# A weight ring of twelve slots of 1 MB in place of six of 2 MB, in an encoder step with 32 experts

## The reference

```python
logits = xt @ w_router + b_router              # 288 x 32
top_val, top_idx = lax.top_k(logits, 4)
gates = softmax weights of the four, 0 elsewhere
for e in range(32):
    gu = xt @ w1[e] + b1[e]                    # w1[e]: 1024 x 2048
    gate = minimum(gu[:, :1024], 7.0)
    up = clip(gu[:, 1024:], -7.0, 7.0)
    act = (up + 1) * (gate * sigmoid(1.702 * gate))
    out = out + gates[:, e:e+1] * (act @ w2[e] + b2[e])   # w2[e]: 1024 x 1024
y = layer_norm(alpha * h1 + out)
```

## Time and profile before

| | |
|---|---|
| three timed runs | 1148.43, 1148.84, 1150.51 us (median 1148.84) |
| profiled execution | 1148.38 us, its span 1146.6 us |
| mean granted PE clock | 0.98 of full speed |
| read from HBM | 420.11 MB |
| PE, DVE, ACT busy | 93%, 36%, 17% of the span |
| ring loads | 192 DMAs of 2 MB |

### The profile page before, as it was taken

One profiled execution on the slowest core, in us unless ns is written; L12 is line 12 of the kernel. 1 busy time (PEld: TensorE's weight loads), 2 busy tenths in 40 slices (PEclk: granted clock), 3 DMA queues, 4 the chain that ended last, 5 costly groups with the idle time before them and its releaser, 6 DMA issues.

```text
span 1146.6 us, 13983 instructions
## 1 busy us (share of the span) xinstructions
PE 1063.8 (93%) x5419; PEld 449.5 (39%) x5420; DVE 407.4 (36%) x692; ACT 193.9 (17%) x432; POOL 17.1 (1%) x25
## 2 busy tenths in 40 slices
PE   8989999889999999999999999999999999999992
PEld 7766565333333333333333333333333333333340
DVE  7683256422222222222222222222222222222227
ACT  3334110111111111111111111111111111111102
POOL 1003000000000000000000000000000000000001
PEclk9999897999999999999999999999999999999997
DMA  9650243999999999999999999999999999999971
GB/s 324 258 221 1 76 183 132 374 386 428 429 429 428 428 428 429 429 430 427 429 428 428 429 429 430 427 429 428 428 429 429 430 426 429 428 428 429 429 297 41
DMA packets 37201, 421.91 MB, mean 368 GB/s; under 512 B 6285, under 2 KB 6925, under 8 KB 12506
## 3 DMA queue, kind: packets, MB, share of 16 engines
q1 hardware_dynamic: 36842, 420.41, 87.4%
q10 hardware_dynamic: 336, 1.18, 0.3%
HBM read 420.11 MB, written 1.46 MB: 368 GB/s over the span
## 4 chain that ended last, share of the span: by engine, by line
DMA 45%; PE 43%; DVE 9%; issue 1%; ACT 1%; SPq 0%; DVEq 0%; ACTq 0%
DMA ring<-in_w_dram 44%; PE ps L817 20%; PE ps L839 7%; PE ps L548 4%; PE ps L662 3%; DVE area L1469 1%; PE ps L859 1%; PE ps L527 1%; PE ps L645 1%; DVE area L1460 1%; DVE area L1463 1%; DVE area L1456 1%; DVE stats L1179 1%; PE ps L762 1%; PE ps L798 1%
## 5 line engine op out<-in xcount | busy, mean ns | idle before, releaser
L817 PE MATMUL ps<-ring,area 128*64 128x512 f32 x2048 | 453.1, 596 | 24.8 <-DMA ring<-in_w_dram 24.0
L817 PEld LDWEIGHTS ps<-ring,area 128*64 128x64 f32 x2048 | 142.0, 137 | 316.1 <-issue 256.2
L839 PE MATMUL ps<-ring,area 128*64 128x512 f32 x1024 | 232.2, 595 | 0.0
L1456 DVE TENSOR_SCALAR area<-ps 128x512 f32<-128x512 f32 x32 | 22.1, 691 | 382.5 <-PE ps L817 382.5
L1469 DVE TENSOR_TENSOR area<-area,ps 128x1024 f32<-128x1024 f32 (+1 forms) x99 | 120.2, 1214 | 57.1 <-PE ps L859 57.1
L839 PEld LDWEIGHTS ps<-ring,area 128*64 128x64 f32 x1024 | 69.7, 136 | 124.5 <-issue 122.1
L1115 ACT ACTIVATE area<-area 128x512 f32<-128x512 f32 x32 | 20.1, 629 | 494.5 <-DVE area L1456 494.5
L859 PE MATMUL ps<-y_sb,giveT 128*128 128x512 f32 x198 | 71.4, 443 | 14.7 <-DVE area L1469 12.3
L1448 DVE SCALAR_TENSOR_TENSOR y_sb<-ps,gcol,y_sb 64x512 fp32r<-64x512 f32 x64 | 48.1, 751 | 101.6 <-ACT y_sb L1087 101.2
L789 PE MATMUL ps<-area 128*64 128x512 bf16 x558 | 66.1, 382 | 2.2 <-DVE area L1383 2.2
L1087 ACT ACTIVATE y_sb<-ps,gcol 64x512 fp32r<-64x512 f32 x64 | 43.8, 684 | 95.4 <-PE ps L839 94.6
(11 more groups left out here) (199 smaller groups left out, 608.6 us busy)
## 6 DMA issues: line engine op xcount, KB each, us to landing
ring<-in_w_dram SPq DMA_DIRECT2D x192, 2048.0 KB, 22.0
area<-in_w_o_dram SPq DMA_DIRECT2D x1, 4096.0 KB, 13.0
area<-in_w_in_dram SPq DMA_DIRECT2D x1, 2560.0 KB, 16.4
area<-in_w_in_dram SPq DMA_DIRECT2D x1, 2336.0 KB, 9.3
area<-in_w_in_dram SPq DMA_DIRECT2D x1, 2048.0 KB, 20.4
lnb<-in_ln_g_dram SPq DMA_DIRECT2D x3, 512.0 KB, 10.3
lnb<-in_ln_b_dram SPq DMA_DIRECT2D x3, 512.0 KB, 11.7
rows<-in_x_prompt_dram SPq DMA_DIRECT2D x2, 512.0 KB, 3.9
```

The source lines that it names most:

```text
L817: last = mm(ps_gu[g * BLK:(g + 1) * BLK, c, :], x[:, spot(k), :], w[:, a:a + 512], start=False, stop=(k == KT - 1))
L839: last = mm(ps_y[g * BLK:(g + 1) * BLK, :], hT[:, c, h, :], w2_t[:, h, c, g * 512:(g + 1) * 512], start=False, stop=(h == 1 and c == 3))
L1456: v.tensor_scalar(g_sb, ps_gu[:, 0, :], LIMIT, None, ALU.min).then_inc(gate, 1)
```

## The change

`SLOT` becomes 2048 float32 for each partition (1 MB a slot) and `NSLOT` 12, so that the ring keeps its 12 MB. Slots 0 to 7 hold one K block of w1 each, slots 8 to 11 two K blocks of w2 each. Every slot has its own DMA, its own semaphore for the landing and its own release. On PE this gives a wait ahead of each of the eight K blocks of w1 and ahead of each pair of K blocks of w2, where there was one ahead of each pair and each half, and a release after each. SP issues twelve DMAs for an expert in place of six, in the same order of bytes; each one reads 8 KB for each partition in place of 16 KB. The loads of expert 0 are split in the same way, at the same places in SP's stream. The buffers carved out of the ring keep their bytes. The matmuls, their order, and the keep-warm matmuls of expert 31 are as before; the waits of DVE and ACT that named slots 3, 4 and 5 now name 7, 8 and 11, so that DVE's `select` (which overwrites `sel`, read by the bias matmuls ahead of slot 8's) may run half a down product sooner.

```diff
-    SLOT = 2 * 2 * F
-    NSLOT = 6
+    SLOT = 2 * F
+    NSLOT = 12
...
-        w1_t = ring[:, 0:4, :].rearrange("p s (k n) -> p (s k) n", k=2)
-        w2_t = ring[:, 4:6, :].rearrange("p s (c n) -> p s c n", c=4)
+        w1_t = ring[:, 0:8, :]
+        w2_t = ring[:, 8:12, :].rearrange("p (h d) (c n) -> p h (d c) n", h=2, c=2)
...
         def w1_part(e, s):
 
-            return w1_v[e, s // 2, :, s % 2 * SLOT:(s % 2 + 1) * SLOT]
+            return w1_v[e, s // 4, :, s % 4 * SLOT:(s % 4 + 1) * SLOT]
+
+        def w2_part(e, s):
+
+            return w2_v[e, s // 2, :, s % 2 * SLOT:(s % 2 + 1) * SLOT]
...
-            for s in range(2):
+            for s in range(4):
                 sp.dma_start(ring[:, s, :], w1_part(0, s)).then_inc(w_in_slot[s], 16)
...
-            for h in range(2):
-                sp.dma_start(ring[:, 4 + h, :], w2_v[0, h]).then_inc(w_in_slot[4 + h], 16)
+            for s in range(4):
+                sp.dma_start(ring[:, 8 + s, :], w2_part(0, s)).then_inc(w_in_slot[8 + s], 16)
...
             def load(e, s):
 
-                src = w1_part(col(e), s) if s < 4 else w2_v[col(e), s - 4]
+                src = w1_part(col(e), s) if s < 8 else w2_part(col(e), s - 8)
                 sp.wait_ge(slot_free[s], e)
                 sp.dma_start(ring[:, s, :], src.rearrange("e p n -> p (e n)")).then_inc(w_in_slot[s], 16)
...
                 for k in range(KT):
-                    if k % 2 == 0:
-                        if free and k > 0 and isinstance(e, int) and e == NE - 1:
-                            keep_warm(7, bank=2)
-                        pe.wait_ge(w_in_slot[k // 2], 16 * (e + 1))
+                    if free and k % 2 == 0 and k > 0 and isinstance(e, int) and e == NE - 1:
+                        keep_warm(7, bank=2)
+                    pe.wait_ge(w_in_slot[k], 16 * (e + 1))
...
-                    if free and k % 2 == 1 and k < KT - 1:
-                        last.then_inc(slot_free[k // 2], 1)
+                    if free and k < KT - 1:
+                        last.then_inc(slot_free[k], 1)
...
-                pe.wait_ge(w_in_slot[4 + h], 16 * (e + 1))
                 for c in range(4):
+                    if c % 2 == 0:
+                        pe.wait_ge(w_in_slot[8 + 2 * h + c // 2], 16 * (e + 1))
...
-                if free:
-                    last.then_inc(slot_free[4 + h], 1)
+                    if free and c % 2 == 1:
+                        last.then_inc(slot_free[8 + 2 * h + c // 2], 1)
...
-                    dve.wait_ge(slot_free[4], e + 1)
+                    dve.wait_ge(slot_free[8], e + 1)
                     select(col(e + 1))
```

More of the change, by code:

```diff
@@ L145, in carve @@
             return base[:, at:at + n]
-        spare = ring[:, 2:6, :].rearrange("p s n -> p (s n)")
+        spare = ring[:, 4:12, :].rearrange("p s n -> p (s n)")
         qiT = carve(spare, 4 * TOK).rearrange("p (i t) -> p i t", i=4)
@@ L154, in encoder_kernel @@
         cache_rows = carve(spare, 2 * P).rearrange("p (c d) -> p c d", c=2)
-        assert used[0] <= SLOT
-        used[0] = SLOT
+        assert used[0] <= 2 * SLOT
+        used[0] = 2 * SLOT
         bias_f = carve(spare, 3 * F)[0:3 * NE, :]
@@ L160, in encoder_kernel @@
         pool_w_sb = carve(spare, 4 * P).rearrange("p (g c) -> p g c", g=4)
-        assert used[0] == 2 * SLOT
+        assert used[0] == 4 * SLOT
         qT = carve(spare, 4 * TOK).rearrange("p (i t) -> p i t", i=4)
@@ L171, in encoder_kernel @@
         probs = carve(spare, 8 * 288)
-        assert used[0] <= 4 * SLOT
+        assert used[0] <= 8 * SLOT
         used[0] = 0
@@ L418, in _ @@
             sp.wait_ge(idx_used, 4 * NT)
-            sp.dma_start(ring[:, 2, :], w1_part(0, 2)).then_inc(w_in_slot[2], 16)
+            for s in (4, 5):
+                sp.dma_start(ring[:, s, :], w1_part(0, s)).then_inc(w_in_slot[s], 16)
             sp.wait_ge(lastu_sb, 1)
@@ L425, in _ @@
             sp.wait_ge(poolmm_ps, 4)
-            sp.dma_start(ring[:, 3, :], w1_part(0, 3)).then_inc(w_in_slot[3], 16)
+            for s in (6, 7):
+                sp.dma_start(ring[:, s, :], w1_part(0, s)).then_inc(w_in_slot[s], 16)
             sp.wait_ge(attT_ps, NT)
@@ L898, in expert @@
                 pe.wait_ge(sel_ready, e + 1)
-                up_products(xT, e, True).then_inc(slot_free[3], 1)
+                up_products(xT, e, True).then_inc(slot_free[7], 1)
                 if isinstance(e, int) and e == 0:
@@ L1129, in expert @@
                 act.wait_ge(giveT_ready, e + 2)
-                act.wait_ge(slot_free[5], e + 1)
+                act.wait_ge(slot_free[11], e + 1)
                 gated_high(y_high)
@@ L1485, in expert @@
                     one_hot(pick, place[:, :, col(e + 1)], first_slots).then_inc(pick_ready, 1)
-                swiglu(slot_free[3], gate_ready, sig_ready, up_ready, prod_ready, e + 1, h_ready)
+                swiglu(slot_free[7], gate_ready, sig_ready, up_ready, prod_ready, e + 1, h_ready)
                 accumulate(0, comb_done[0], e + 1, acc_done[0])
```

## The result

Four executions of the changed kernel took 1157.15 to 1160.09 us, median 1157.68, beside 1149.09 for the kernel before; the ratio is 1.0072, interval 1.0059 to 1.0085. The profiled execution took 1157.20 us with a span of 1155.4, 8.8 more than before. The forecast was 1155.9, slower by 7.5 us.

The account below looks back on a forecast made before the run. The prediction took the saturated stream of DMA loads to bound the kernel: 1148.38 us - 1.7 (restart) + 11.0 (stream) - 1.8 (tail) = 1155.9 us, +0.65%. Its own range was 1153 to 1159.5, for 8 in 10 1148 to 1160.5.

Parts of the forecast that it names:

- What bounds the kernel: From 300 us on DMA is full at 428 to 429 GB/s; start of unbroken loads, their megabytes and the tail set the time.
- The stream: Experts 3 to 29 and w1 of expert 30: 332 MB at 0.033 us more per MB for smaller packets, +11.0 us.
- Three lines: Straight lines through the 16 KB packet and one of 4.1, 2.6 or 2 KB: fixed part 7.2, 8.7 or 9.4 ns.
- The middle line: The line through the 398 GB/s stretch, its packets taken as 2560 bytes: a fixed part of 8.7 ns for each packet.
- The restart: Expert 3's slot 0 load, after the 255 us hole, is issued at 254.2 in place of 255.90: -1.7 us.
- the entry into the loop: PE stands still 3.77 us on entering its loop, before expert 2, then runs at clock 0.50 from 250 to 253 us.
- The tail: After the last wait, in w1's last quarter, 8 records are left on PE in place of 16: -1.8 us.
- What costs nothing: Six more PE waits for each expert, SP's extra issues, unchanged SBUF use, matmuls and byte order add no time to the sum.
- packets of 8 KB are free: Rival: bytes alone set the stream's rate at this size, only the two gains are left, 1144.9 us; chance 0.13.
- the read pattern: Rival: w1 reads of 8 KB out of each 32 KB slow the stream to 398 GB/s, near 1207 us; chance 0.04.
- the open latency: Rival: each DMA's fixed latency shows, 1 us for each of 166 further DMAs, 1322 us; chance 0.01.
- Half the price: Rival: smaller packets cost the stream 15 to 20 ns for 1 MB, 1149.9 to 1151.5 us; chance 0.12.

Follow-up runs that it names:

- padded run: The kernel before with 32 already satisfied waits put into PE's expert 0, shifting PE's code, nothing else changed: 1147.19 us, ratio 0.9979.
- the same waits in the changed kernel: The changed kernel with 32 already satisfied waits put into PE's expert 0: 1157.48 us, ratio 1.0065 to the kernel before.
- pairs: The changed kernel's 1 MB loads, but PE waits for and releases slots two at a time as before: 1160.41 us, ratio 1.0101 to the kernel before.

## Why the prediction was right

**What bounds the kernel.** Right. The stream of loads sets the time from 255 us to the last wait; in each experiment the time of an expert followed the packets alone, and no edit of PE's waits or code moved it.

**The stream** (11.0 us): right in mechanism, sized a little low, 12.6 measured. The step is the price of a packet. Three lines gave 7.2, 8.7 and 9.4 ns, and I took a value between them, 8.2; here a packet costs 9.4. The line through the 4 KB stretch was the low one, and it drew the value down because it was nearest in size. Its 158.3 ns for a packet came from a stretch of 6.5 us; a whole stream at 4 KB takes 30.72 us / 192 = 160.0, and with that the same line gives (4 x 160.0 - 611.6) / 3 = 9.5 ns. An error of 1% in the short stretch (6.5 us, not the 10 that the rivals speak of) was a quarter of the answer. The middle line was misread too: the 739 packets of that stretch that aren't tiny carry 1.99 MB, 2.7 KB each and not 2560 bytes, and with that it gives 9.3 ns. The completions, left out of the sum, cost nothing.

**The restart** (-1.7): -2.05, near by luck in part. The half slot gave 1.4 (from PE's resuming to the issue it takes 253.85 - 249.62 = 4.23 us, and 255.90 - 250.26 = 5.64 before). The rest is PE reaching expert 2 0.64 us earlier (249.62 against 250.26), which no term foresaw: the kernel before has a small standstill in expert 1 that the changed one lacks.

```profile
221.08 11.80 PE L817 MATMUL ps<-ring,area 128*64 128x512 f32 x53 [0.75 <-issue]
```

That DMA would be idle anyway, so that earlier gains add nothing, was right as well. The reason given for the standstill, the entry into the loop, was wrong: it doesn't need a loop, and 32 instructions move it. It did the forecast no harm only because the changed code left it where it was. The "within 1 us" I gave it held for this edit and not for others: with the standstill moved into expert 1, the way from PE's start to the last wait came out 0.7 us shorter (padded run), 0.5 longer (the same waits in the changed kernel) and 0.4 longer than expected (pairs), but one that came up on the tail cost 7.2.

**The tail** (-1.8): -1.7, and the run by pairs has the 16 records back.

**What costs nothing**: right in that it cost nothing. In 480 to 1080 us, where rows 3 had 20 waits of up to 1.2 us, PE waits 55 times for the ring (us in total, times, longest), and the clock stays at 1.00:

```profile
PE ps L822 <- DMA ring<-in_w_dram: 23.3, 55, 0.6
```

The prediction had two pieces of idle time in each expert, 1.6 us together; there are three in most, 0.16, 0.55 and 0.55, ahead of K blocks 5, 6 and 7.

**The rivals.** That packets of 8 KB are free is excluded by the run that has them and nothing else; the read pattern and the open latency likewise, since 2 MB loads whose rows are read in one stretch of 16 KB take the same 29.82 us. Half the price, 4 to 5 ns, is excluded by the measured 9.4.

## What to carry to other kernels

Where a stream of loads sets the time, count its packets: megabytes times packets per megabyte times the fixed part of each is what a finer ring costs, and it is paid on every byte, while a finer release or wait pays only at the two ends of the stream, once each, and only if the other engine isn't itself late there. So before halving a slot, see whether the engines ever wait for it anywhere but at those ends. And when an edit changes an engine's code, look for standstills of that engine that nothing released: one of them on the tail cost 7 us here. Last, before two recorded spans are compared, see whether they agree up to the part that was changed: here PE's start differed by up to 4.4 us between executions.

## What the runs showed that was not expected

The fixed part of a packet is the same from 4 to 32 KB to within the reading, 9.4 ns, and a DMA's completion adds nothing that can be read to a full stream.

The clock of PE in 130 to 145 us falls in some executions and not in others with PE just as busy, and moves everything behind it by 3 to 4 us.

PE has standstills of 2.1 to 4.5 us (and some of under 1 us) that need no entry into a loop: in front of expert 2, inside expert 1 or in front of experts 30 or 31, as the code lies. Those over 3 us were followed by a stretch at a clock of 0.50 (250 to 253 us of the changed kernel is one), the one of 2.65 us by none; the one of 2.49 us (the run by pairs) was followed by a lower clock, 0.66 on average over these five microseconds:

```profile
217.00:222.00 5.00, 4.53 (x14) 1.95 (x15) 0.00 (x0) 0.00 (x0) 0.00 (x0) 0.66 0.80 326
```

What PE waits for in them is not shown.
